# Feed-forward network: all gate and up slabs first, then the down projection by output chunk

## The chip, the core and the metric

The kernel runs on one core of one Trainium2 chip, in one launch. The metric is the device time of that launch in microseconds. The engines are TensorE (PE, matrix products into PSUM), VectorE (DVE), ScalarE (ACT), GpSimd (POOL) and SyncE (SP), which here only issues transfers. TensorE's weight loads have a row of their own in the profile (PEld).

## What is computed

Three transformer layers on one sequence of 256 tokens, width 1024, all in float32. The first has a stick-breaking and a differential attention side by side, the second a forgetting attention, the third a low-rank attention; each ends with the same feed-forward network, and the third is followed by a last normalization. The change touches only the three feed-forward networks:

```python
D_MODEL, SEQ = 1024, 256
D_FF = ((8 * D_MODEL // 3 + 255) // 256) * 256        # 2816 = 22 chunks of 128
def swiglu(xn, w_gate, w_up, w_down):
    return (jax.nn.silu(xn @ w_gate) * (xn @ w_up)) @ w_down
h = h + swiglu(rmsnorm(h, ffn_norm[l]), w_gate[l], w_up[l], w_down[l])
...
return rmsnorm(h, final_norm)
```

## The kernel before

**Slabs.** All weights lie in HBM as a row of slabs of 128 partitions x 1024 float32 (512 KB), numbered in the order of their use. Each slab goes through four steps: SyncE loads it into one of six slots of `stage`; ScalarE rounds it to a high part `w_hi` (`split_hi`, L1016, or `next_hi`, L1032); VectorE subtracts to get the low part `w_lo` (`split_lo`, `next_lo`, L1485); TensorE multiplies (L426). Activations are kept transposed, features on partitions and 256 tokens along the row, and are split in the same way, high and low. One block of 128x128 weights needs three products of 256 columns: high by high, high by low, low by high. Where the two parts of the activations stand side by side (`a_pair`), the first two are one product of 512 columns; its two halves come out in the two halves of a PSUM bank and are added later (`wide_slab`). The other form (`by_weights`) adds all three into the same 256 columns.

**Order of the work.** The order on each engine is written out by hand; engines wait for each other by counting semaphores: `loaded` (a transfer has landed), `hi_made`, `lo_made`, `slab_done` (TensorE is done with a slab). The load of slab n waits for `lo_made` of slab n-6, since they share a slot of `stage`. ScalarE's split of slab n+6 waits for `slab_done` of slab n, VectorE's low split that is written beside slab n is that of slab n+4.

**The feed-forward network.** 66 slabs in 11 rounds of six: gate, up, gate, up, down, down. A gate slab holds the weights of one of 22 chunks of 128 hidden features, for all 1024 inputs; an up slab the same. After them ScalarE copies out the low half of the bank (`low_out`, L1219), VectorE adds the halves (L1688) and multiplies by the row factor `rB` of the normalization (L1478), ScalarE does the silu (L1210), VectorE multiplies by the up part, and the result is split again (`ff_high`, L1214, `ff_low`, L1485). A down slab holds the 128 rows of one chunk, for all 1024 outputs: it adds into all eight output chunks, which stay in four PSUM banks (`acc`, banks 0 to 3) for the whole network (`row_slab`). Only two gated chunks exist at a time. The rounds 1 to 9 are loops on the engines (`Fori`), the first and the last are written out. At the end VectorE adds the eight sums to `xT` (L1515) and makes the low parts of the next stage's input, ScalarE its high parts (`norm_start`); TensorE begins the next stage's first two slabs block by block as these come in (`first_column_slabs`).

Of the kernel before, what the change touches and what calls it, by code (L numbers as in the profile page):

```python
# [18 lines left out]
P = 128  # L19
TOK = 256  # L20
D = 1024
NC = D // P
DFF = ((8 * D // 3 + 255) // 256) * 256
NG = DFF // 256
# [62 lines left out]
MLA_LAST = 14  # L87


def trunk(nc, xT_d, slab_d, vec_d, con_d, pos_d, out_d):  # L90
    f32, f32r, i32 = mybir.dt.float32, mybir.dt.float32r, mybir.dt.int32
    ALU, ACT = mybir.AluOpType, mybir.ActivationFunctionType
    with ExitStack() as ctx:
# [5 lines left out]

        stage = sb("stage", [P, SLOTS, SLAB])  # L100
# [5 lines left out]
        arena = sb("arena", [P, 10240])  # L106
# [24 lines left out]
        def chunks(t, a, n):  # L131
# [18 lines left out]
        ff_hi, ff_lo = chunks(arena_r, 0, 2), chunks(arena_r, 512, 2)  # L150
# [48 lines left out]
                                 "do_taken", "dms_done", "dr_ready", "dn_ready", "do_hi", "do_lo"))  # L199
        mix_ready, mhi_ready, mlo_ready = sem("mix_ready"), sem("mhi_ready"), sem("mlo_ready")  # L200
# [16 lines left out]
        fin_made, pool_added = sem("fin_made"), sem("pool_added")  # L217
# [106 lines left out]
        outT, gained, squared = chunks(arena, 0, 8), chunks(arena, 2048, 8), chunks(arena, 4096, 8)  # L324
# [6 lines left out]
        def _(sp):  # L331
# [33 lines left out]
            def ffn_loads(base, first=0):  # L365

                for n in range(base, base + 5):
                    load(n, n - first)
                with sp.Fori(0, NG - 1) as i:
                    for c, shift in enumerate((1, 1, -2, 0, 0, 0)):  # L370
                        n = base + 5 + c
                        sp.wait_ge(lo_made, i * SLOTS + (n + 1 - SLOTS))
                        sp.dma_start(stage[:, n % SLOTS, :],
                                     slab_d[bass.ds(i * SLOTS + (n + shift - first), 1)].rearrange("a p n -> p (a n)")
                                     ).then_inc(loaded[n % SLOTS], 16)
                load(base + 6 * NG - 1, base + 6 * NG - 1 - first)
# [40 lines left out]
            for i, (c, count) in enumerate(OUT_PARTS[:-1]):  # L417
                sp.wait_ge(out_ready, i + 1)
                sp.dma_start(out_d[:, c:c + count, :], outT[:, c:c + count, :]).then_inc(out_done, 16)
# [4 lines left out]
        def _(pe):  # L424
# [337 lines left out]
            def ff(p):  # L762
                return ff_hi[:, p, :], ff_lo[:, p, :]

            def ffn_round(f, base, i, last=False):

                n, q = base - 1 + 6 * i, 22 * f + 2 * i
                slot = [(base - 1 + c) % SLOTS for c in range(6)]
                for p in range(2):
                    pe.wait_ge(gu_taken, q + p - 1)  # L770
                    wide_slab(n + 3 * p, slot[3 * p], bank[4 + 2 * p])
                    pe.wait_ge(ff_made, q + p - 1)
                    if last and p:
                        column_slab(n + 4, slot[4], half(7, 0))
                    else:
                        wide_slab(n + 3 * p + 1, slot[3 * p + 1], bank[5 + 2 * p])
                    if p == 0:
                        pe.wait_ge(fflo_ready, q)
                        row_slab(n + 2, slot[2], *ff(1), False)
                if last:  # L780
                    last_rows(n + 5, [ff(0), ff(1)],
                              *([(done, q + 1), (done, q + 2)] for done in (ffhi_ready, fflo_ready)))
                    return
                pe.wait_ge(fflo_ready, q + 1)
                row_slab(n + 5, slot[5], *ff(0), False)

            def ffn(f, base):
                q = 22 * f
                if f:
                    pe.wait_ge(ff_made, q)  # L790
                first_column_slabs(base, [half(4, 0), half(5, 0)], 2 * f + 1)
                norm_sum(2 * f + 1)
                wide_slab(base + 2, (base + 2) % SLOTS, bank[6])
                pe.wait_ge(r_ready, 2 * f + 2)
                wide_slab(base + 3, (base + 3) % SLOTS, bank[7])
                pe.wait_ge(fflo_ready, q + 1)
# [194 lines left out]
            pe.wait_ge(ff_made, 22 * 3)  # L991
            for i, pair in enumerate((sumsq[:, :], sq[:, 0:TOK])):
                pe.wait_ge(fin_added, i + 1)
                mm(half(7, 0), ones, pair, i == 0)
            pe.wait_ge(pool_added, 1)
            mm(half(7, 0), ones, sq[:, TOK:2 * TOK], False)
            for c in (6, 7):
                pe.wait_ge(fin_squared, c + 1)
                last = mm(half(7, 0), ones, squared[:, c, :], False)
            last.then_inc(sum_done, 1)  # L1000
# [3 lines left out]
        def _(act):  # L1004
# [13 lines left out]
            def next_hi(n):  # L1018
                m = n + SLOTS
                if m < NSLAB:  # L1020
                    act.wait_ge(slab_done, n + 1)
                    act.wait_ge(loaded[m % SLOTS], 16 * (m // SLOTS + 1))
                    if m in UQ_STEP:
                        step = UQ_STEP[m]
                        if step[0] == "R":
                            for i in (m + 1, m + 2):
                                act.wait_ge(loaded[i % SLOTS], 16 * (i // SLOTS + 1))
# [34 lines left out]

            def norm_start(m):

                for c in range(NC):
                    act.wait_ge(x_ready, 8 * (m - 1) + c + 1)
# [1182 lines left out]
```

## Time and profile before

| | us |
|---|---|
| median of 3 runs | 1009.96 (1009.61 to 1009.97) |
| profiled execution, span | 1007.6 |
| TensorE busy | 993.9 (99%) |
| TensorE weight loads | 923.4 (92%) |
| VectorE busy | 714.1 (71%) |
| ScalarE busy | 607.8 (60%) |
| queue of SyncE's transfers | 52.9% of 16 engines |

The median of the runs lies 2.4 us above the span of the profiled execution. Busy time counts instructions in flight; TensorE's products overlap, so its own progress is read from the start times in its timeline. "Share" of a DMA queue is the time that its packets took, over the time of all 16 DMA engines. TensorE's granted clock is full (1.0) over the whole run but for the last microseconds.

### The profile page before, as it was taken

Reading aid. Unit: us, or ns where it says so; the run is one execution under the profiler, and the core shown is the slowest. Engines: PE = TensorE matmul, PEld = TensorE weight load, DVE = VectorE, ACT = ScalarE, POOL = GpSimd, SP = SyncE. Lnnn points to the kernel's source line nnn. Section 1 sums busy time; section 2 is a strip of 40 time slices with the busy share of each in tenths; the row PEclk is TensorE's granted clock in tenths of the full one; section 3 lists DMA queues with packets and bytes.
Section 4 is the critical chain, followed back from the end, with each engine's and each line's share of the span. In section 5 each row is a group of like instructions: output and inputs, shape, how many; then the busy total and the mean of one; then the engine's idle time right before and its main releaser. Section 6 shows DMA issues by size and latency. Waiting matters only on the chain.

```text
span 1007.6 us, 19765 instructions
## 1 busy us (share of the span) xinstructions
PE 993.9 (99%) x7214; PEld 923.4 (92%) x7214; DVE 714.1 (71%) x1360; ACT 607.8 (60%) x1094; POOL 59.6 (6%) x79
## 2 busy tenths in 40 slices
PE   8999999999999999999999999999999999999997
PEld 8999989999999999989999999999989999999996
DVE  4668987776666668666496666668977686666665
ACT  5677785575555556565475555557768675555553
POOL 3011110120000002000020000002200010000000
PEclk9999999999999999999999999999999999999999
DMA  7743445466555554433545556564665456565631
GB/s 292 273 149 110 153 145 187 148 206 190 176 181 186 183 189 159 157 127 127 167 146 188 187 187 187 187 187 127 203 194 191 146 167 188 187 187 187 187 125 43
DMA packets 50904, 174.05 MB, mean 173 GB/s; under 512 B 6304, under 2 KB 8864, under 8 KB 50720
## 3 DMA queue, kind: packets, MB, share of 16 engines
q1 hardware_dynamic: 49664, 172.12, 52.9%
q10 hardware_dynamic: 1184, 1.18, 0.6%
q8 instruction: 36, 0.59, 0.2%
q14 instruction: 20, 0.16, 0.0%
HBM read 169.86 MB, written 1.05 MB: 170 GB/s over the span
## 4 chain that ended last, share of the span: by engine, by line
PE 90%; DVE 5%; ACT 2%; DMA 1%; issue 1%; SPq 0%; DVEq 0%; ACTq 0%
PE bank L426 89%; DVE w_lo L1485 2%; PE bank L647 1%; DVE a_pair L1504 1%; DMA stage<-slab_dram 1%; DVE xT L1515 1%; DVE arena L1478 0%; ACT w_hi L1032 0%; ACT a_pair L1067 0%; DVE soft_s L1566 0%; ACT soft_p L1124 0%; ACT w_hi L1016 0%; DVE tmp L1478 0%; DVE tmp L1712 0%; DVE arena_r L1485 0%
## 5 line engine op out<-in xcount | busy, mean ns | idle before, releaser
L426 PE MATMUL bank<-a_pair,w_hi 128*128 128x256 f32 (+1 forms) x1992 | 537.8, 342 | 2.8 <-DVE w_lo L1485 2.7
L426 PE MATMUL bank<-a_pair,w_lo 128*128 128x256 f32 x1488 | 417.6, 282 | 0.0
L1485 DVE TENSOR_TENSOR w_lo<-stage,w_hi 128x1024 fp32r<-128x1024 f32 (+2 forms) x322 | 387.4, 1211 | 8.4 <-ACT w_hi L1016 3.5
L426 PEld LDWEIGHTS bank<-a_pair,w_hi 128*128 128x128 f32 x1992 | 343.4, 190 | 48.6 <-DVE w_lo L1485 4.0
L426 PE MATMUL bank<-arena_r,w_hi 128*128 128x256 f32 x1792 | 328.8, 284 | 0.4 <-DVE arena_r L1485 0.2
L426 PEld LDWEIGHTS bank<-arena_r,w_hi 128*128 128x128 f32 x1792 | 278.4, 191 | 5.6 <-DVE arena_r L1485 1.4
L426 PEld LDWEIGHTS bank<-a_pair,w_lo 128*128 128x128 f32 x1488 | 283.1, 190 | 0.0
L426 PE MATMUL bank<-arena_r,w_lo 128*128 128x256 f32 x896 | 252.7, 283 | 0.0
L1016 ACT ACTIVATE w_hi<-stage 128x1024 fp32r<-128x1024 f32 x192 | 202.4, 1055 | 33.4 <-PE bank L426 33.4
L1032 ACT ACTIVATE w_hi<-stage 128x1024 fp32r<-128x1024 f32 (+2 forms) x126 | 128.0, 1026 | 79.5 <-PE bank L426 69.7
L426 PEld LDWEIGHTS bank<-arena_r,w_lo 128*128 128x128 f32 x896 | 171.0, 191 | 0.0
L1688 DVE TENSOR_TENSOR tmp<-bank,arena 128x256 f32<-128x256 f32 x123 | 51.9, 422 | 160.3 <-ACT arena L1219 160.3
L1219 ACT ACTIVATE arena<-bank 128x256 f32<-128x256 f32 x123 | 47.1, 383 | 163.2 <-PE bank L426 163.2
L2088 POOL TENSOR_TENSOR sumsq<-sumsq,sq 128x256 f32<-128x256 f32 x47 | 38.5, 820 | 644.3 <-ACT sq L1053 591.8
L1478 DVE TENSOR_TENSOR tmp<-tmp,rB 128x256 f32<-128x256 f32 x129 | 54.4, 422 | 4.8 <-ACT tmp L1210 2.7
L1214 ACT ACTIVATE arena_r<-tmp 128x256 fp32r<-128x256 f32 x66 | 27.6, 418 | 43.5 <-DVE tmp L1478 35.7
L426 PE MATMUL bank<-w_hi,a_pair 128*128 128x256 f32 x256 | 47.7, 287 | 0.0
L426 PEld LDWEIGHTS bank<-w_hi,a_pair 128*128 128x128 f32 x256 | 39.8, 191 | 0.9 <-issue 0.6
L426 PE MATMUL bank<-w_lo,a_pair 128*128 128x256 f32 x128 | 36.2, 282 | 0.0
L1566 DVE CUSTOM_DVE_ANT_0 soft_s<-bank,con 128x128 f32<-128x128 f32 x80 | 25.1, 355 | 15.5 <-PE bank L426 15.4
L1154 ACT ACTIVATE soft_p<-soft_s,small 128x128 f32<-128x128 f32 x64 | 31.2, 491 | 4.0 <-DVE small L1619 3.2
L1504 DVE SCALAR_TENSOR_TENSOR a_pair<-xT,vec,a_pair 128x256 fp32r<-128x256 f32 x48 | 28.7, 604 | 6.5 <-ACT a_pair L1282 5.1
(185 smaller groups left out, 674.8 us busy)
## 6 DMA issues: line engine op xcount, KB each, us to landing
stage<-slab_dram SPq DMA_DIRECT2D x319, 512.0 KB, 4.2
con<-con_dram SPq DMA_DIRECT2D x1, 1153.5 KB, 10.6
xT<-xT_dram SPq DMA_DIRECT2D x4, 256.0 KB, 5.5
arena<-arena ACTq DMA_DIRECT2D x1, 1024.0 KB, 8.9
arena<-tmp SPq DMA_DIRECT2D x32, 32.0 KB, 3.2
out_dram<-arena SPq DMA_DIRECT2D x3, 256.0 KB, 2.4
tmp<-arena SPq DMA_DIRECT2D x16, 16.0 KB
vec<-vec_dram SPq DMA_DIRECT2D x1, 213.5 KB, 11.5
```

Source lines behind the costliest of these rows:

```text
L426: return nc.tensor.matmul(out, lhsT, rhs, start=start, stop=True, skip_group_check=True)
L1016: nc.scalar.activation(w_hi[:, slot, :], stage[:, slot, :], ACT.Copy).then_inc(hi_made, 1)
L1032: nc.scalar.activation(hi, raw, ACT.Copy).then_inc(hi_made, 1)
L1154: last = nc.scalar.activation(soft_p[:, g % 2, cols], soft_s[:, g % 2, cols], ACT.Exp, scale=0.125 if g < HEADS else rq_col[:, t:t + 1], b ...
L1214: nc.scalar.activation(ff_hi[:, p, :], tmp[:, 4 + p, :], ACT.Copy).then_inc(ffhi_ready, 1)
L1219: nc.scalar.activation(low[:, i, :], half(4 + (0, 2, 1, 3)[i], 1), ACT.Copy).then_inc(low_taken, 1)
L1478: return nc.vector.tensor_tensor(out, a, b, ALU.mult)
L1485: return nc.vector.tensor_tensor(out, a, hi.bitcast(f32), ALU.subtract)
L1504: return nc.vector.scalar_tensor_tensor(out, x, g, hi.bitcast(f32), ALU.mult, ALU.subtract)
L1566: return nc.vector.tensor_tensor_reduce(out=s[:, cols], in0=b[:, cols], in1=con[:, mask + cols.start:mask + cols.stop], scale=1.0, scalar= ...
L1688: return nc.vector.tensor_tensor(out, half(b, 0), low[:, i, :], ALU.add)
L2088: nc.gpsimd.tensor_tensor(sumsq[:, :], sumsq[:, :], sq[:, (i % 2) * TOK:(i % 2 + 1) * TOK], ALU.add).then_inc(sq_added, 1)
```

## The change

Each feed-forward network now runs its 44 gate and up slabs one after another, in eight PSUM banks in turn (`GU_BANK`), and keeps all 22 gated chunks, high and low part side by side (`ff_pair`): 12 in `arena_r`, 10 in `ff_more`, which lies over `arena`. The down projection then runs output chunk by output chunk: 8 columns of 22 blocks, each block one product of 512 columns and one of 256. The very last column of the third network keeps the three products of 256. The weights in HBM are laid out as before. A slab of eight down blocks is put together by the transfers: each block is 128 rows of 128 numbers (512 B) out of a different row slab, and 22 such slabs take 38 transfers. After each column VectorE adds the two halves of its bank to `xT`, and ScalarE and VectorE make the next stage's input for that chunk while the next column runs. The loops on the engines are gone.

```diff
+NF = 2 * NG
+GU_BANK = (4, 5, 6, 0, 1, 2, 3, 7)
+DOWN_BANK = (4, 0, 1, 2, 3, 7, 5, 6)
+DOWN = 2 * NF
+DOWN_END = {(NF * c + NF - 1) // NC: c for c in range(NC)}
+KEPT = 12
...
+        def down_order(c):
+            if c:
+                return [*range(0, NF, 2), *range(1, NF, 2)]
+            return [*range(0, NF - 2, 2), *range(1, NF - 2, 2), NF - 2, NF - 1]
...
             def ffn_loads(base, first=0):
-                for n in range(base, base + 5):
-                    load(n, n - first)
-                with sp.Fori(0, NG - 1) as i:
-                    for c, shift in enumerate((1, 1, -2, 0, 0, 0)):
...
+                for t in range(DOWN):
+                    load(base + t, base - first + 6 * (t // 4) + t % 4)
+                rows = slab_d[base - first:base - first + 6 * NG].rearrange("(i s) p n -> p i s n", s=6)
+                for s in range(NF):
+                    n = base + DOWN + s
+                    sp.wait_ge(lo_made, n - SLOTS + 1)
+                    for c, j, k, count in down_runs(s):
+                        sp.dma_start(
+                            span(stage[:, n % SLOTS, :], k * P, count * P).rearrange("p (i n) -> p i n", n=P),
+                            rows[:, j // 2:j // 2 + count, 4 + j % 2, c * P:c * P + P]).then_inc(loaded[n % SLOTS], 16)
...
+            def down_columns(f, base):
+                for c in range(NC):
+                    b = bank[DOWN_BANK[c]]
+                    plain = f == 2 and c == NC - 1
...
+                    for i, j in enumerate(down_order(c)):
+                        s, k = divmod(NF * c + i, NC)
+                        n, w = base + DOWN + s, slice(k * P, k * P + P)
+                        if k == 0:
+                            pe.wait_ge(lo_made, n + 1)
...
+                        if plain:
+                            last = by_weights(n % SLOTS, k * P, b[:, 0:TOK], ff_hi(j), ff_lo(j), i == 0)
+                        else:
+                            mm(b[:, :], w_hi[:, n % SLOTS, w], ff_pair(j), i == 0)
+                            last = mm(b[:, 0:TOK], w_lo[:, n % SLOTS, w], ff_hi(j), False)
...
             def ffn(f, base):
-                q = 22 * f
+                q = NF * f
                 if f:
                     pe.wait_ge(ff_made, q)
                 first_column_slabs(base, [half(4, 0), half(5, 0)], 2 * f + 1)
                 norm_sum(2 * f + 1)
-                wide_slab(base + 2, (base + 2) % SLOTS, bank[6])
-                pe.wait_ge(r_ready, 2 * f + 2)
-                wide_slab(base + 3, (base + 3) % SLOTS, bank[7])
-                pe.wait_ge(fflo_ready, q + 1)
-                row_slab(base + 4, (base + 4) % SLOTS, *ff(0), True)
-                with pe.Fori(1, NG - 1) as i:
-                    ffn_round(f, base, i)
-                ffn_round(f, base, NG - 1, last=True)
+                for t in range(2, DOWN):
+                    if t == 7:
+                        pe.wait_ge(r_ready, 2 * f + 2)
+                    if t >= 8:
+                        pe.wait_ge(ff_made if t % 2 else gu_taken, q + t // 2 - 3)
+                    wide_slab(base + t, (base + t) % SLOTS, bank[GU_BANK[t % 8]])
+                down_columns(f, base)
...
+                for j in range(1, NF):
+                    gate(f, j)
+                    ff_low(f, j - 1)
+                    next_lo(base + 2 * j)
+                    silu_out(f, j)
+                    up(f, j)
+                    next_lo(base + 2 * j + 1)
+                ff_low(f, NF - 1)
+                for s in range(NF):
+                    c = DOWN_END.get(s)
+                    if c is not None:
+                        down_residual(f, base, c)
+                    next_lo(base + DOWN + s)
+                    if c is not None and f < 2:
+                        norm_low(2 * f + 2, c)
```

TensorE, before, in the loop of the first network: the last block of an up slab and the start of the down slab behind it.

```order
1135 L426 MATMUL bank<-a_pair,w_hi 128x512
1136 L426 MATMUL bank<-a_pair,w_lo 128x256
1137 L784 REGISTER_ALU
1138 L487 REGISTER_ALU
1139 L426 MATMUL bank<-arena_r,w_hi 128x256 x2
1140 L426 MATMUL bank<-arena_r,w_lo 128x256
1141 L426 MATMUL bank<-arena_r,w_hi 128x256 x2
1142 L426 MATMUL bank<-arena_r,w_lo 128x256
```

TensorE, now, at the end of the 44th gate/up slab of the first network and the start of the first down column (`arena_r` holds the first twelve gated chunks, `ff_more` the others).

```order
1672 L479 MATMUL bank<-a_pair,w_hi 128x512
1673 L479 MATMUL bank<-a_pair,w_lo 128x256
1674 L479 MATMUL bank<-arena_r,w_hi 128x512
1675 L479 MATMUL bank<-arena_r,w_lo 128x256
...
1684 L479 MATMUL bank<-arena_r,w_hi 128x512
1685 L479 MATMUL bank<-arena_r,w_lo 128x256
1686 L479 MATMUL bank<-ff_more,w_hi 128x512
1687 L479 MATMUL bank<-ff_more,w_lo 128x256
```

A block of down weights was three products of 256 columns and is one of 512 and one of 256.

SyncE's queue, before, in the loop of the first network: one load per slab.

```order
35 L373 ISA
36 L373 DMA stage<-slab_dram 128x1024
37 L373 ISA
38 L373 DMA stage<-slab_dram 128x1024
39 L369 REGISTER_ALU
40 L369 COMPARE_AND_BRANCH
41 L353 DMA stage<-slab_dram 128x1024 x38
```

SyncE's queue, now, where the down slabs of the first network begin (partitions x blocks x numbers).

```order
20 L406 DMA stage<-slab_dram 128x1024 x64
21 L427 DMA stage<-slab_dram 128x8x128
22 L427 DMA stage<-slab_dram 128x2x128
23 L427 DMA stage<-slab_dram 128x6x128
24 L427 DMA stage<-slab_dram 128x4x128
25 L427 DMA stage<-slab_dram 128x128 x2
26 L427 DMA stage<-slab_dram 128x2x128
27 L427 DMA stage<-slab_dram 128x8x128
```

A down slab is no longer 128 rows of 4 KB but eight blocks of 128 rows of 512 B, in one to four transfers.

## Rows read from the trace of the kernel before

**Rows 1.** Page: engines (busy us, share, instructions); chain by engine and line.
```profile
PE 993.9 (99%) x7214; PEld 923.4 (92%) x7214; DVE 714.1 (71%) x1360; ACT 607.8 (60%) x1094; POOL 59.6 (6%) x79
...
PE bank L426 89%; DVE w_lo L1485 2%; PE bank L647 1%; DVE a_pair L1504 1%; DMA stage<-slab_dram 1%; DVE xT L1515 1%; DVE arena L1478 0%; ACT w_hi L1032 0%; ACT a_pair L1067 0%; DVE soft_s L1566 0%; ACT soft_p L1124 0%; ACT w_hi L1016 0%; DVE tmp L1478 0%; DVE tmp L1712 0%; DVE arena_r L1485 0%
```
**Rows 2.** TensorE's timeline: start, us, engine line op, tiles, shapes, count.
```profile
604.81 0.40 PE L426 MATMUL bank<-arena_r,w_hi 128*128 128x256 f32 x2
...
607.68 0.40 PE L426 MATMUL bank<-a_pair,w_hi 128*128 128x512 f32 x1
...
613.34 0.40 PE L426 MATMUL bank<-arena_r,w_hi 128*128 128x256 f32 x2
```
**Rows 3.** TensorE's timeline, start and end of FFN 1, start of FFN 2.
```profile
199.33 0.28 PE L426 MATMUL bank<-a_pair,w_hi 128*128 128x256 f32 x1
...
205.34 0.58 PE L426 MATMUL bank<-a_pair,w_hi 128*128 128x512 f32 x1
...
211.35 0.51 PE L426 MATMUL bank<-arena_r,w_hi 128*128 128x256 f32 x2
...
214.33 0.40 PE L426 MATMUL bank<-a_pair,w_hi 128*128 128x512 f32 x1
...
387.79 0.28 PE L426 MATMUL bank<-a_pair,w_hi 128*128 128x256 f32 x1
...
513.35 0.50 PE L426 MATMUL bank<-a_pair,w_hi 128*128 128x512 f32 x1
...
519.44 0.50 PE L426 MATMUL bank<-arena_r,w_hi 128*128 128x256 f32 x2 [0.18 <-DVE arena_r L1485]
```
**Rows 4.** Stretch 390 to 395: each engine's busy us (instructions), clock, DMA share, GB/s.
```profile
390.00:395.00 5.00, 5.00 (x44) 4.92 (x44) 4.97 (x7) 4.87 (x9) 2.74 (x4) 1.00 0.00 0
```
**Rows 5.** Timeline of all engines, the tail; in brackets the idle time before.
```profile
998.78 0.75 DVE L1515 TENSOR_TENSOR xT<-xT,bank 128x256 f32<-128x256 f32 x2 [0.35 <-PE bank L426]
...
999.95 1.03 PE L426 MATMUL bank<-arena,con 128*128 128x256 f32 x4
1001.01 0.47 ACT L1036 ACTIVATE rB<-bank,con 128x256 f32<-128x256 f32 x1 [0.23 <-PE bank L426]
```
**Rows 6.** Groups by line and shape: busy us, mean ns of one, idle before.
```profile
L1485 DVE TENSOR_TENSOR w_lo<-stage,w_hi 128x1024 fp32r<-128x1024 f32 x305 | 373.2, 1231 | 6.4 <-ACT w_hi L1016 3.5 <-ACT w_hi L1032 2.6
...
L1016 ACT ACTIVATE w_hi<-stage 128x1024 fp32r<-128x1024 f32 x192 | 202.4, 1055 | 33.4 <-PE bank L426 33.4
...
L1688 DVE TENSOR_TENSOR tmp<-bank,arena 128x256 f32<-128x256 f32 x123 | 51.9, 422 | 160.3 <-ACT arena L1219 160.3
...
L1219 ACT ACTIVATE arena<-bank 128x256 f32<-128x256 f32 x123 | 47.1, 383 | 163.2 <-PE bank L426 163.2
...
L1515 DVE TENSOR_TENSOR xT<-xT,bank 128x256 f32<-128x256 f32 x48 | 19.0, 413 | 14.3 <-PE bank L426 14.3
```
**Rows 7.** Page, DMA issues: KB of one, median us from issue to landing.
```profile
stage<-slab_dram SPq DMA_DIRECT2D x319, 512.0 KB, 4.2
```
**Rows 8.** DMA by stretch (packets, MB, share of engines); 0:3, 17:19, 19:21, 211:399, 727:739.
```profile
GB/s 0 0 0 0 0 0 0 0 0 0 0 0 0 0 0 0 0 0 0 0 0 0 0 0 51 68 85 82 28 72 79 55 218 273 218 273 273 300 300 191
...
DMA packets 373, 0.78 MB, mean 388 GB/s; under 512 B 43, under 2 KB 250, under 8 KB 373
q1 hardware_dynamic: 373, 0.78, 105.1%
...
DMA packets 223, 0.82 MB, mean 410 GB/s; under 512 B 26, under 2 KB 26, under 8 KB 222
q1 hardware_dynamic: 222, 0.80, 100.1%
...
DMA packets 9371, 34.16 MB, mean 182 GB/s; under 512 B 1042, under 2 KB 1042, under 8 KB 9368
q1 hardware_dynamic: 9368, 34.11, 57.8%
...
q10 hardware_dynamic: 1040, 1.05, 49.9%
```

More of the change, by code:

```diff
@@ L149, in trunk @@
         ob_hi, ob_lo = chunks(arena_r, 2048, 4), chunks(arena_r, 3072, 4)
[L150 removed]
+        ff_first = span(arena_r, 0, KEPT * 2 * TOK).rearrange("p (c n) -> p c n", n=2 * TOK)
         fo_hi, fo_lo = chunks(arena_r, 0, 8), chunks(arena_r, 2048, 8)
@@ L322, in add_index, with ff_pair, ff_hi, ff_lo @@
             return 7 * m + (6 if m > 4 else 0)
-        outT, gained, squared = chunks(arena, 0, 8), chunks(arena, 2048, 8), chunks(arena, 4096, 8)
+        gained, squared = chunks(arena, 5120, 8), chunks(arena, 7168, 8)
+        def ff_pair(j):
+            return ff_first[:, j, :] if j < KEPT else ff_more[:, j - KEPT, :]
+        def ff_hi(j):
+            return ff_pair(j)[:, 0:TOK]
+        def ff_lo(j):
+            return ff_pair(j)[:, TOK:2 * TOK]
+        def down_order(c):
+            if c:
+                return [*range(0, NF, 2), *range(1, NF, 2)]
+            return [*range(0, NF - 2, 2), *range(1, NF - 2, 2), NF - 2, NF - 1]
+        def down_runs(s):
+            runs = []
+            for k in range(NC):
+                c, i = divmod(NC * s + k, NF)
+                j = down_order(c)[i]
+                if runs and runs[-1][0] == c and runs[-1][1] + 2 * runs[-1][3] == j:
+                    runs[-1][3] += 1
+                else:
+                    runs.append([c, j, k, 1])
+            return runs
+        def loads_of(n):
+            s = [n - base - DOWN for base in (FFN1, FFN2, FFN3) if base + DOWN <= n < base + 6 * NG]
+            return len(down_runs(s[0])) if s else 1
+        def all_loads(n):
+            return 16 * sum(loads_of(m) for m in range(n % SLOTS, n + 1, SLOTS))
+        def column_ended(engine, f, base, c):
+            if c in (3, 7):
+                engine.wait_ge(slab_done, base + DOWN + (NF * (c + 1)) // NC)
+            else:
+                engine.wait_ge(down_done, 6 * f + c + 1 - c // 4)
         OUT_PARTS = ((0, 1), (1, 2), (3, 2), (5, 2), (7, 1))
@@ L990, in _ @@
             ffn(2, FFN3)
[L991 to L1000, printed above, removed]
+            pe.wait_ge(fin_added, NC - 2)
+            mm(half(7, 0), ones, sumsq[:, :], True)
+            pe.wait_ge(fin_squared, NC)
+            mm(half(7, 0), ones, squared[:, NC - 1, :], False).then_inc(sum_done, 1)
         @block.scalar
@@ L1455, in _ @@
             ffn(2, FFN3)
-            for c in range(NC):
-                act.wait_ge(x_ready, 8 * 5 + c + 1)
-                nc.scalar.activation(squared[:, c, :], xT[:, c, :], ACT.Square).then_inc(fin_squared, 1)
-                for i in {5: (0,), 7: (6, 7)}.get(c, ()):
-                    nc.scalar.activation(gained[:, i, :], xT[:, i, :], ACT.Copy, scale=gain(6, i)).then_inc(fin_made, 1)
             norm_end(6)
@@ new lines, in ff_low, with ffn @@
+            def ff_low(f, j):
+                dve.wait_ge(ffhi_ready, NF * f + j + 1)
+                minus_hi(ff_lo(j), tmp[:, 4 + j % 2, :], ff_hi(j)).then_inc(fflo_ready, 1)
+            def ffn(f, base):
+                next_lo(base)
+                next_lo(base + 1)
+                dve.wait_ge(r_ready, 2 * f + 2)
+                plain_gate(base, NF * f)
+                silu_out(f, 0)
+                plain_up(base + 1, NF * f)
+                for j in range(1, NF):
[6 more added lines that the diff above has]
+                ff_low(f, NF - 1)
+                for s in range(NF):
+                    c = DOWN_END.get(s)
+                    if c is not None:
+                        down_residual(f, base, c)
+                    next_lo(base + DOWN + s)
+                    if c is not None and f < 2:
+                        norm_low(2 * f + 2, c)
+                    if c is not None and f == 2 and c < NC - 1:
+                        dve.wait_ge(x_ready, 8 * 5 + c + 1)
+                        nc.vector.tensor_scalar(gained[:, c, :], xT[:, c, :], gain(6, c), None, ALU.mult
+                                                ).then_inc(fin_gained, 1)
+                        add_square(c)
```

267 lines of the change are left out of this document (93 added, 174 removed).

## The prediction

> **What bounds the kernel now.** I read the page first, then TensorE's timeline, then the DMA view in stretches, then the engines' groups by shape. The page shows one bound: TensorE is busy for 99% of the span, and the chain of waits runs over its product line for 89% of it [rows 1]. In TensorE's timeline the FFN is a strict beat. A gate or up slab (eight 512-column products and eight of 256) starts at 607.68, two of them last until 613.34: 5.66 us, 2.83 each. A down slab (24 products of 256 columns) starts at 604.81 and lasts until 607.68: 2.87 us, and over the whole loop a round of two gate/up slabs and one down slab is 8.53 us, so 2.88 fits better than 2.87 [rows 2]. So both forms stream the same 768 columns for each weight block, and the wide form costs 0.05 us less per slab. The first FFN takes 199.33 to 387.79, 188.46 us [rows 3].
>
> Nothing else is on the path there. At the hand-over from the first FFN to the next stage (390 to 395) TensorE is busy for all 5.00 us although VectorE and ScalarE are full and no load moves [rows 4]. So the end-of-FFN residuals are already hidden, and taking them out of that place gives no time.
>
> **The change part by part.**
>
> 1. Down slabs in the wide form. 66 slabs (22 in each of three FFNs), 0.05 us each: 3.3 us. The very last column keeps the old form, 22 blocks x 0.36 instead of 0.353: 0.15 us back. Three up slabs that were plain (24 products) become wide: 0.15 us. Sum 3.3 us gained.
>
> 2. The first down slab no longer stands behind the first gated chunk. In before, slabs 3 and 4 take 205.34 to 211.35, 6.01 us where two wide slabs take 5.66; the next slab takes 2.98 where 2.88 is usual [rows 3]. So 0.35 + 0.1 us is a wait for the first chunk's low part. In after the fifth slab is a gate slab that wants only its weights. The second FFN shows 513.35 to 519.44, 6.09 us, in the same place [rows 3], and the third the same. Gain 3 x 0.45 to 0.55: 1.4 us.
>
> 3. The tail. In before the two last residual adds stand in a row from 998.78, then the square and the closing product at 999.95, and ScalarE starts on the norm at 1001.01 [rows 5]. In after only one output chunk waits for the last slab: one add of about 0.4 us less. Gain 0.4 us.
>
> 4. VectorE. For each pair of gate/up slabs it makes two low splits (2 x 1.23 us), five products or sums of 256 columns and one low part of the chunk, 0.42 us each: 2.46 + 2.52 = 4.98 us [rows 6], beside 5.66 us of TensorE. Before, a down slab came in between and gave it 8.53 us for 6.2. It is 88% full now, so it keeps up, with 0.68 us for its waits. I take zero. The low split it has to deliver is for the slab four further on, over 8 us away, so a single late step is absorbed; only a mean over 5.66 would cost. ScalarE has 2 x 1.06 + 2 x 0.38 [rows 6] and two more of about 0.42: 3.7 us, loose. In the down phase VectorE gets 16 adds of 0.41 us [rows 6] and 8 low parts per FFN, while its 22 splits take 27 of the 62 us: hidden. PSUM: a bank is used again after eight slabs, and what frees it is asked for three chunks back; no wait. The residuals that go away from the hand-over were hidden (above): zero.
>
> 5. The transfers. This is where the change can lose. A gate/up slab still moves in 128 pieces of 4 KB. A down slab is now 1024 pieces of 512 B, in 38 transfers for 22 slabs. The issue costs nothing: fewer than two a slab, and one transfer of 1024 pieces of 1 KB (arena to arena) is already there. What one slab may take is TensorE's 2.83 us, since the loads go one behind another. A load is issued when the slab six earlier has been split and is wanted about 8 us later in the gate/up phase; with 4.2 us from issue to landing [rows 7] about 4 us are spare, once per FFN. So the loss per FFN is 22 x (L - 2.83) - 4 us, L being one slab's transfer, and nothing when that is negative.
>
> L is not in the trace. Its nearest rows: from 19 to 21 the queue is full with 4 KB pieces and moves 410 GB/s; from 17 to 19 it is as full, with 330 data pieces (373 less 43 small) of 2.36 KB on average, most of them 1 to 1.7 KB, and moves 388 GB/s [rows 8]. On 16 engines that is 160 ns for 4096 B and 97 ns for 2364 B: 0.036 ns per byte and 12 ns for each piece. A piece of 512 B comes to 31 ns, 64 per engine to 2.0 us. In the FFN itself the queue is occupied 57.8% for 182 GB/s, that is 315 GB/s when occupied and not 410 [rows 8], so the same stretch by 1.3: 2.6 us. I take L = 2.6 us: under 2.83, hidden, with 8% of room. The low end, bytes alone, is 512 KB at 410 GB/s: 1.3 us. The high end is the arena-to-arena transfer: 1040 pieces of 1 KB occupy 49.9% of 16 engines for 12 us, 92 ns each [rows 8]. If that price went with the piece and not with the byte, 64 of them are 5.9 us.
>
> The Trainium skill (DMA: Bandwidth & Descriptors, Why small descriptors are slow) gives a fixed cost of about 3 cycles per packet beside one per 32 bytes: 19 cycles for 512 B, against 131 for 4 KB, so 16% more for a slab. By that rule, scaled from the 1.3 us of the rows, L would be 1.5 us; the two windows make it 2.0, so the trace finds more cost than the rule.
>
> Sum: 3.3 + 1.4 + 0.4 = 5.1 us. The profiled span is 1007.6; the median of the runs is 1009.96, 2.4 us above it, and I keep that distance. Span 1002.5, time 1004.9 us.
>
> **Rivals.**
>
> A. Pieces are supplied no faster than one per 3 to 4 ns, whatever their size. For: the very first transfer (128 pieces of 256 B) runs at 51 to 85 GB/s with the engines far from full [rows 8], 3.0 ns a piece at best and about 3.9 in the mean (32 KB in 0.5 us). Against: it is the first one, cold, and 1 KB pieces ran back to back. Then L is 3.1 to 4.0; with 3.5 the loss is 3 x (22 x 0.67 - 4) = 32 us: 1037 us. It decides from L = 3.1, where the loss (2 us per FFN) eats the gain. TensorE would idle in the down phase, waiting for VectorE's low split, which waits for ScalarE's split, which waits for the load. The same holds if scattered reads of one 512 B column out of 4 KB rows lower the memory's rate by a third or more.
> [...]
>
> B. The arena price, L = 5.9: 3 x (22 x 3.07 - 4) = 191 us: 1196 us. Against: that transfer reads and writes on-chip memory at the same time, the new ones only write it.
>
> C. VectorE becomes the bound in the gate/up phase: its order (gate, low part, split, rescale, up, split) waits for ScalarE twice per pair. If each pair takes one ScalarE split more (1.06 us), a pair is 6.0 and not 5.66: 21 x 3 x 0.35 = 22 us: 1027 us. Against: ScalarE is busy 3.7 of 5.66.
>
> D. No change: small stalls of the first down slabs give the 5 us back: 1009 to 1011 us.
>
> **How the numbers follow.** Forecast (1003 to 1008) 0.58; A 0.26, of which a third lies above 1040; B 0.03; C 0.05; D 0.08. What a measurement of this kernel can tell from no change is about 0.2%, 2 us. Faster 0.60 (the forecast and the smallest part of A), same 0.09, slower 0.31. The forecast's own range is 1003 to 1008; the range that holds 8 in 10 goes up into A: 1002.5 to 1040.
>
> **What would show it.** Right: in the down phase TensorE's 512- and 256-column products alternate without a gap, 2.83 us per slab; the DMA share there rises from 0.58 towards 0.9; issue to landing of the 512 B slabs under 8 us; each FFN about 186.8 us. Wrong by A: VectorE's low split as TensorE's releaser and, behind it, ScalarE waiting on the slab load, a DMA share near 1 (or a rate near 3 ns per piece with a lower share). Wrong by C: low splits late in the gate/up phase, where the loads are old ones.

## The result, and the profile after

The changed kernel takes 1001.17 us (median of 4 runs, 1000.99 to 1002.94) against 1009.97 us (1009.61 to 1010.71): a ratio of 0.9917, 95% interval 0.9903 to 0.9931. Forecast were 1004.9 us, range 1002.5 to 1040: the sign was right, the gain was 8.8 us and not 5.1, and the time lies 1.3 us below the range. The profiled execution has a span of 999.5 us at a time of 1001.25.

The page of the changed kernel, engines and chain, which answers to [rows 1]:

```profile
PE 985.7 (99%) x6678; PEld 893.9 (89%) x6678; DVE 736.7 (74%) x1392; ACT 594.7 (59%) x1095; POOL 58.1 (6%) x78
...
PE 95%; DVE 2%; ACT 1%; DMA 1%; issue 0%; SPq 0%; DVEq 0%; ACTq 0%
```

TensorE is still the bound, with fewer products. TensorE's timeline of the changed kernel where stages begin (start, us, then the instruction; answers to [rows 3]): `a_pair` at 128x256 opens an FFN (feed-forward network) or the stage behind it, `arena_r` at 128x512 the down columns, `sumsq` the tail.

```profile
199.27 0.28 PE L479 MATMUL bank<-a_pair,w_hi 128*128 128x256 f32 x1
...
321.94 0.39 PE L479 MATMUL bank<-arena_r,w_hi 128*128 128x512 f32 x1
...
382.95 0.28 PE L479 MATMUL bank<-a_pair,w_hi 128*128 128x256 f32 x1
...
502.11 0.28 PE L479 MATMUL bank<-a_pair,w_hi 128*128 128x256 f32 x1
...
627.32 0.40 PE L479 MATMUL bank<-arena_r,w_hi 128*128 128x512 f32 x1
...
689.50 0.28 PE L479 MATMUL bank<-a_pair,w_hi 128*128 128x256 f32 x1
...
802.83 0.28 PE L479 MATMUL bank<-a_pair,w_hi 128*128 128x256 f32 x1
...
990.80 0.59 PE L479 MATMUL bank<-sumsq,con 128*128 128x256 f32 x2
```

The same starts in the kernel before, as far as [rows 3] doesn't have them:

```profile
506.95 0.28 PE L426 MATMUL bank<-a_pair,w_hi 128*128 128x256 f32 x1
...
695.88 0.28 PE L426 MATMUL bank<-a_pair,w_hi 128*128 128x256 f32 x1
...
809.26 0.28 PE L426 MATMUL bank<-a_pair,w_hi 128*128 128x256 f32 x1
...
998.59 0.38 PE L426 MATMUL bank<-sumsq,con 128*128 128x256 f32 x1
```

Differences of such starts, in both traces:

| stage | before, us | after, us | saved |
|---|---|---|---|
| FFN 1 | 188.46 | 183.68 | 4.78 |
| second layer's attention | 119.16 | 119.16 | 0 |
| FFN 2 | 188.93 | 187.39 | 1.54 |
| third layer's attention | 113.38 | 113.33 | 0.05 |
| FFN 3 | 189.33 | 187.97 | 1.36 |
| tail | 9.0 | 8.7 | 0.25 |

The sum is 8.0 of the 8.1 us by which the spans differ. The second and third FFN save about what was forecast (some 1.6 each). The first saves 3.3 us more. Its down phase takes 61.01 us (321.94 to 382.95) where the second's takes 62.18 (627.32 to 689.50), with the same instructions. The reason is in the smallest rows. First the changed kernel in FFN 1 and in FFN 2, TensorE's timeline:

```profile
259.54 0.39 PE L479 MATMUL bank<-a_pair,w_hi 128*128 128x512 f32 x1
259.77 0.28 PE L479 MATMUL bank<-a_pair,w_lo 128*128 128x256 f32 x1
259.89 0.39 PE L479 MATMUL bank<-a_pair,w_hi 128*128 128x512 f32 x1
...
520.26 0.40 PE L479 MATMUL bank<-a_pair,w_hi 128*128 128x512 f32 x1
520.50 0.28 PE L479 MATMUL bank<-a_pair,w_lo 128*128 128x256 f32 x1
520.61 0.40 PE L479 MATMUL bank<-a_pair,w_hi 128*128 128x512 f32 x1
520.84 0.28 PE L479 MATMUL bank<-a_pair,w_lo 128*128 128x256 f32 x1
520.96 0.40 PE L479 MATMUL bank<-a_pair,w_hi 128*128 128x512 f32 x1
```

Then the kernel before, the same view, in the first two wide slabs of FFN 1 and in a loop round of FFN 2:

```profile
206.91 0.39 PE L426 MATMUL bank<-a_pair,w_hi 128*128 128x512 f32 x1
207.14 0.28 PE L426 MATMUL bank<-a_pair,w_lo 128*128 128x256 f32 x1
207.26 0.39 PE L426 MATMUL bank<-a_pair,w_hi 128*128 128x512 f32 x1
...
608.04 0.40 PE L426 MATMUL bank<-a_pair,w_hi 128*128 128x512 f32 x1
608.28 0.28 PE L426 MATMUL bank<-a_pair,w_lo 128*128 128x256 f32 x1
608.40 0.40 PE L426 MATMUL bank<-a_pair,w_hi 128*128 128x512 f32 x1
```

A wide block (512 and 256 columns) has two beats, a beat being the distance from the start of one block to the start of the next. In the fast one it is 346.7 ns throughout (mean of 510 blocks of FFN 1; 230 ns from the start of the wide product to that of the narrow one, then 117). In the slow one the mean is 353.3 ns (998 blocks of FFN 2 and 3), in a cycle of three blocks, about 350, 361 and 349. The record of the 512-column product shows it at a glance: 0.39 us in the fast beat, 0.40 in the slow one. In the kernel before all loop rounds have the slow beat, which is the 2.83 us per slab that I read from [rows 2]; only the first two wide slabs of FFN 1 have the fast one. The granted clock is the same, as the stretches of the changed kernel show (from:to, length, busy us and instructions of PE, PEld, DVE, ACT, POOL, then clock, DMA share, GB/s): two of gate/up slabs in FFN 1 and 2, one of down columns.

```profile
213.00:321.00 108.00, 108.00 (x625) 95.25 (x624) 91.34 (x160) 64.31 (x119) 0.00 (x0) 1.00 0.63 191
329.00:382.00 53.00, 53.00 (x308) 46.73 (x307) 33.25 (x40) 25.34 (x33) 4.77 (x6) 1.00 0.68 202
517.00:625.00 108.00, 108.00 (x613) 93.64 (x612) 89.54 (x154) 62.65 (x116) 0.00 (x0) 1.00 0.63 190
```

TensorE is "busy" for all 108 us in both stretches and does 625 products in one, 613 in the other: 2% that neither TensorE's busy share nor the clock shows. (The granted clock was 0.5 from 7.9 to 11.3 us and in the last microseconds, in both kernels and outside all three FFNs.)

The waits of FFN 1 in the changed kernel (210 to 382), the costliest three (us in total, times, longest):

```profile
POOL sumsq L2099 <- ACT sq L1102: 165.5, 6, 131.5
ACT arena L1270 <- PE bank L479: 44.1, 40, 1.4
DVE xT L1560 <- PE bank L479: 18.9, 7, 3.6
```

None of that view's rows has TensorE as the one that waits; at the start of FFN 2 its weight load waits once for a low split, 0.4 us. VectorE is 85% busy in the gate/up phase (91.34 of 108) and late for nothing. The tail, all engines' timeline (answers to [rows 5]), now has one add:

```profile
991.00 0.42 DVE L1561 TENSOR_TENSOR xT<-xT,bank 128x256 f32<-128x256 f32 x1 [6.13 <-PE bank L479]
...
992.66 0.47 ACT L1085 ACTIVATE rB<-bank,con 128x256 f32<-128x256 f32 x1 [0.39 <-PE bank L479]
```

The transfers while only down slabs are loaded (325 to 360) and the page's row on a whole slab (answers to [rows 7]):

```profile
DMA packets 13554, 6.80 MB, mean 194 GB/s; under 512 B 336, under 2 KB 13552, under 8 KB 13552
...
q1 hardware_dynamic: 13552, 6.77, 69.6%
...
stage<-slab_dram SPq DMA_DIRECT2D x277, 512.0 KB, 4.0
```

The queue is occupied 0.696 x 35 us for 6.77 MB: 1.89 us for a slab of 0.524 MB. (The loads run ahead of TensorE: in a window up to 380 a third of the bytes would be the next stage's 4 KB pieces.)

### The profile page after: what moved, and what is told of

Read it like the earlier page. It is cut to its first block, busy times and chain, and to the rows that moved or that the text cites. A ratio compares the mean times of both kernels' runs of the same rounds, so it can differ in the third digit from the quotient of the medians.

```text
span 999.5 us, 17282 instructions
## 1 busy us (share of the span) xinstructions
PE 985.7 (99%) x6678; PEld 893.9 (89%) x6678; DVE 736.7 (74%) x1392; ACT 594.7 (59%) x1095; POOL 58.1 (6%) x78
## 4 chain that ended last, share of the span: by engine, by line
PE 95%; DVE 2%; ACT 1%; DMA 1%; issue 0%; SPq 0%; DVEq 0%; ACTq 0%
PE bank L479 94%; PE bank L700 1%; DMA stage<-slab_dram 1%; DVE w_lo L1512 1%; DVE arena L1505 0%; ACT w_hi L1081 0%; DVE soft_s L1601 0%; ACT soft_p L1175 0%; DVE soft_p L1629 0%; DVE arena L1872 0%; ACT arena L1096 0%; DVE arena L1905 0%; ACT arena L1095 0%; DVE soft_p L1625 0%; DVE arena L1870 0%
## 5 line engine op out<-in xcount | busy, mean ns | idle before, releaser
L479 PE MATMUL bank<-a_pair,w_hi 128*128 128x512 f32 (+1 forms) x1968 | 533.7, 343 | 2.2 <-DVE w_lo L1512 2.1
L1081 ACT ACTIVATE w_hi<-stage 128x1024 fp32r<-128x1024 f32 (+2 forms) x314 | 326.5, 1044 | 140.0 <-PE bank L479 128.0
L479 PE MATMUL bank<-arena_r,w_hi 128*128 128x256 f32 (+1 forms) x1036 | 239.1, 315 | 0.0
L479 PE MATMUL bank<-arena_r,w_lo 128*128 128x256 f32 x656 | 184.6, 282 | 0.0
L479 PEld LDWEIGHTS bank<-arena_r,w_hi 128*128 128x128 f32 x1036 | 170.1, 190 | 14.0 <-issue 1.4
L479 PEld LDWEIGHTS bank<-arena_r,w_lo 128*128 128x128 f32 x656 | 125.0, 191 | 0.0
L479 PE MATMUL bank<-ff_more,w_hi 128*128 128x512 f32 (+1 forms) x250 | 86.5, 387 | 0.0
L479 PE MATMUL bank<-ff_more,w_lo 128*128 128x256 f32 x240 | 67.4, 281 | 0.0
L479 PEld LDWEIGHTS bank<-ff_more,w_hi 128*128 128x128 f32 x250 | 46.3, 188 | 10.3
L479 PEld LDWEIGHTS bank<-ff_more,w_lo 128*128 128x128 f32 x240 | 45.4, 189 | 0.0
```

The source lines that it names most:

```text
L479: return nc.tensor.matmul(out, lhsT, rhs, start=start, stop=True, skip_group_check=True)
L1081: nc.scalar.activation(hi, raw, ACT.Copy).then_inc(hi_made, 1)
```

## The experiments

**The transfers alone.** `e1_rows4k` keeps everything but loads a down slab as 128 whole rows (the down weights are then the wrong ones, the amount of work is the same).

```diff
-                    for c, j, k, count in down_runs(s):
-                        sp.dma_start(
-                            span(stage[:, n % SLOTS, :], k * P, count * P).rearrange("p (i n) -> p i n", n=P),
-                            rows[:, j // 2:j // 2 + count, 4 + j % 2, c * P:c * P + P]).then_inc(loaded[n % SLOTS], 16)
+                    sp.dma_start(stage[:, n % SLOTS, :], rows[:, s // 2, 4 + s % 2, :]).then_inc(loaded[n % SLOTS], 16)
```

> The changed kernel, but each down slab is loaded as whole rows of 4 KB in one transfer (the down weights of a block are then wrong ones; the work on all engines is the same). If the gathered transfers are hidden, 1001.2 us as the changed kernel, within 1 us. If they cost something, or if the 8 us gained come partly from lighter memory traffic, it differs by more than 2 us; my prediction's rival A (pieces are supplied at 3 to 4 ns each) would make this one faster by several us.

Measured: 1001.3 us (997.28, 1001.49, 1001.41, 1001.18), the time of the changed kernel. The run of 997.28 is the profiled one, and in it FFN 2 has the fast beat too (625 products in 517 to 625). It lies some 4 us below the other three: one FFN is 510 blocks x 6.6 ns = 3.4 us, and most of the rest is in the third layer's attention, 112.65 us here and 113.33 in the changed kernel. Its transfers from 325 to 360:

```profile
q1 hardware_dynamic: 1899, 6.89, 62.3%
```

That is 1.66 us per slab. The pieces of 512 B cost 0.23 us of queue per slab and nothing in time.

**The product form alone.** `e2_down256` keeps the new order and transfers, and gives every down column the three products of 256.

```diff
-                    plain = f == 2 and c == NC - 1
+                    plain = True
...
-                if f < 2 or c < NC - 1:
-                    chain(nc.vector.tensor_tensor(xT[:, c, :], xT[:, c, :], half(DOWN_BANK[c], 1), ALU.add))
```

> The changed kernel, but every down column in three products of 256 columns (one add per column at its end). My theory of two beats (a wide block takes 346.7 ns in one state of TensorE, 353.3 in another, and the first FFN of the changed kernel was in the fast one): the first FFN loses 22 x 8 x 13.3 ns = 2.3 us, the others 154 and 176 blocks x 6.7 ns = 1.2 and 1.0 us: 1005.7 us. The prediction's single price of 0.05 us a slab: 1001.2 + 3.1 = 1004.3 us. Rival, the gain is in the gate and up slabs standing together and not in the form: no difference, 1001 us.

Measured: 1005.13 us (1003.13 to 1006.79), ratio 0.9959 (0.9945 to 0.9973), so the form is worth some 4 us of the 8.8. The two expectations with a gain from the form, 1004.3 and 1005.7 us, both lie within the spread of the runs; it only excludes that the form gains nothing. In the profile (1003.13) the down columns of FFN 2 run from 629.99 to 693.35: 176 blocks in 63.36 us, 360 ns each, without spread and with no fast or slow variant. Against them the changed kernel's wide columns take 62.18 (slow) or 61.01 (fast). The gate/up slabs of FFN 1 are fast here too: FFN 1 takes 186.02 us, 2.4 less than before with the down weights in the old form. So most of that FFN's surplus comes from the gate/up slabs standing together. In this profile those of FFN 3 are fast as well, worth 336 blocks x 6.6 ns = 2.2 us.

**The loops.** `e3_before_straight` is the kernel before with its loops written out on all engines (TensorE's edit; the others are alike).

```diff
-                with pe.Fori(1, NG - 1) as i:
+                for i in range(1, NG - 1):
                     ffn_round(f, base, i)
```

> The kernel before, its loops on the engines written out. Theory of two beats: the row form (256, 256, 256) ahead of each gate slab puts TensorE into the slow beat each time, loop or not, so 1010 us as before. Rival, the loops' branches and registers cost the 6.6 ns per wide block: 42 x 3 x 8 x 6.6 ns = 6 us less, about 1003 us.

Measured: 1009.94 us over 10 runs against 1009.41, ratio 1.0008 (0.9999 to 1.0018), and the slow beat in all the rounds behind the first (only the two wide slabs ahead of FFN 1's and FFN 2's first down slab are fast). Neither the loops nor their branches cost time, and they don't bring the slow beat.

**What flips the beat.** `e4_probe` puts, ahead of six gate slabs per FFN, one or two more products of various widths into the bank that the slab then starts anew.

```diff
...
+                for cols in extra:
+                    mm(out[:, 0:cols], w_hi[:, slot, 0:P], a_pair[:, 0, 0:cols], True)
```

> The changed kernel with extra products of 32 to 512 columns ahead of some gate slabs (every sixth slab of each FFN), into the bank that the slab is about to start, so without effect on the result. Each adds 0.05 to 0.5 us of its own. Two beats as a state that an interruption can change: the beat of the wide blocks (512 plus 256 columns) flips between 346.7 and 353.3 ns behind some of the sizes, in the first FFN from fast to slow and in the others from slow to fast. Rival, the beat belongs to the FFN (its addresses, its code, its traffic): no flip, 346.7 in the first and 353.3 ns in the others throughout.

Measured: 999.50 us, one run. In the trace, F for 346.7 and S for 353.3 ns from there to the next: FFN 1 begins F, then 256 F, 128 **S**, 64 F, 512 F, 192 F, 384 F. FFN 2 begins S, then 256 S, 128 S, 64 **F**, 512 **S**, 192 S, 384 **F**. FFN 3 begins F, then 256+256 F, 320 F, 32 F, 448 F, 128+128 **S**, 96 **F**. One extra product of 64 columns, TensorE's timeline of that kernel in FFN 2:

```profile
555.14 0.40 PE L479 MATMUL bank<-a_pair,w_hi 128*128 128x512 f32 x1
555.38 0.28 PE L479 MATMUL bank<-a_pair,w_lo 128*128 128x256 f32 x1
555.50 0.50 PE L479 MATMUL bank<-a_pair,w_hi 128*128 128x64 f32 x2
555.85 0.28 PE L479 MATMUL bank<-a_pair,w_lo 128*128 128x256 f32 x1
```

The rival is excluded. The beat is a state that in these traces changes only where something breaks the alternation, and not each time; it goes through from the gate/up slabs into the down columns. The extra costs 0.11 us: 555.50 to 555.85 is 0.35 where a 512-column product takes 0.24.

**One extra product per FFN.** `e5_settle` is the changed kernel with a 64-column product ahead of the fifth gate/up slab of each FFN.

```diff
+                if settle:
+                    mm(out[:, 0:64], w_hi[:, slot, 0:P], a_pair[:, 0, 0:64], True)
...
-                    wide_slab(base + t, (base + t) % SLOTS, bank[GU_BANK[t % 8]])
+                    wide_slab(base + t, (base + t) % SLOTS, bank[GU_BANK[t % 8]], t == 4)
```

> The changed kernel with one extra product of 64 columns ahead of the fifth slab of each FFN (0.11 us each, no effect on the result). The probe showed that behind an extra product of 64 (twice), 32, 96 or 384 columns the beat was fast, whatever it was before. Theory of two beats: all three FFNs run at 346.7 ns per block to their end; two FFNs more in the fast beat give 2 x 500 x 6.6 ns = 6.6 us less than a run with one of them fast: 994.8 us, and the runs agree more closely. Rival, the beat of FFN 2 and 3 is drawn anew by something that comes later than this: 1001 us on the mean, runs between 994 and 1004.

Measured: 995.38 us (995.12, 998.96, 994.99, 997.71, 995.38), ratio 0.987 (0.9851 to 0.9888): 5.8 us below the changed kernel by the medians, and the fastest of all here. The stretches of all three FFNs (gate/up) have the fast beat's count:

```profile
213.00:321.00 108.00, 108.00 (x625) 1.00 0.64 191
517.00:625.00 108.00, 108.00 (x625) 1.00 0.65 192
815.00:922.00 107.00, 107.00 (x620) 1.00 0.65 192
```

FFN 2 enters slow and is fast from the extra on (514.9), FFN 3 from 812.8. The FFNs take 183.80, 184.20 and 184.91 us, so the second and third are 3.2 and 3.1 us shorter than in the changed kernel, as 494 and 472 blocks x 6.67 ns, less 0.11 for the extra, demand (3.2 and 3.0). Bringing the fast beat to the other two FFNs gains in each what FFN 1 had beyond them: this shows the beat as the cause of the surplus. Two of the five runs lie 2.6 and 3.8 us above the lowest group, so the runs don't agree more closely, as the expectation had it.

**The same extra in the kernel before.** `e6_before_settle` has it at each gate slab behind a down slab, 20 per FFN, with the loops written out.

```diff
...
-                    wide_slab(n + 3 * p, slot[3 * p], bank[4 + 2 * p])
+                    wide_slab(n + 3 * p, slot[3 * p], bank[4 + 2 * p], True)
```

> The kernel before with its loops written out and one extra product of 64 columns ahead of each gate slab that follows a down slab (20 per FFN). Theory: the two wide slabs behind it run at 346.7 ns and not 353.3, 16 x 6.6 = 0.11 us less, for 0.11 us that the extra product costs: the time stays at 1009 to 1011 us and only the beat changes. Rival, the slow beat of the kernel before belongs to its banks or to VectorE's and ScalarE's reads: the beat stays 353.3 ns and the time rises by 6.6 us.

Measured: 1012.68 us, one run. In the trace the pairs of gate/up slabs are fast and slow in turn (fast from 223.2, 240.4, 257.5, slow between), which neither the theory nor its rival had. 60 extras x 0.11 us cost 6.6, some 30 pairs x 16 blocks x 6.6 ns give back 3.2: 3.4 us more than before, and 3 were measured. So the old order can run fast too, but there each down slab breaks the alternation and a single extra holds for 16 blocks only.

**Smaller pieces.** `e7_pieces256` halves each piece of the changed kernel's down slabs, 2048 of 256 B per slab.

```diff
...
-                            rows[:, j // 2:j // 2 + count, 4 + j % 2, c * P:c * P + P]).then_inc(loaded[n % SLOTS], 16)
+                        for h in (0, 64):
...
+                                rows[:, j // 2:j // 2 + count, 4 + j % 2, c * P + h:c * P + h + 64]
```

> The changed kernel with each 512 B piece of a down slab split into two of 256 B, 2048 pieces a slab. It asks how near the transfers are to the bound. By the per-piece price of 12 ns and 0.036 ns per byte, 128 x 21 = 2.7 us per slab, by the 1.3 for interruptions 3.5 us: 3 x (22 x 0.7 - 4) = 34 us slower, 1035 us. By what the changed kernel's trace shows for a 512 B slab (68% of 2.77 us occupied, 1.9 us), less 0.036 x 512 x 64 = 1.2 us for the bytes, 0.7 us is for 1024 pieces, so 2.6 us here: hidden, 1001 us. By a supply of one piece per 3 ns (rival A): 6 us a slab, 3 x (22 x 3.4 - 4) = 212 us slower.

Measured: 1001.48 us (1001.37, 998.12, 1001.59, 1001.75), no loss. Its transfers from 325 to 360:

```profile
DMA packets 27802, 6.98 MB, mean 200 GB/s; under 512 B 27799, under 2 KB 27799, under 8 KB 27799
...
q1 hardware_dynamic: 27799, 6.94, 102.5%
```

That is 2.71 us per slab, just under the 2.77 that TensorE takes (over 100% of share means that the times of packets overlap): the queue is full almost all the time, and these transfers are hidden with nothing to spare. So 4 KB, 512 B and 256 B pieces occupy the queue for 1.66, 1.89 and 2.71 us. The Trainium skill (DMA: Bandwidth & Descriptors, Why small descriptors are slow) counts 3 cycles per packet beside one per 32 bytes, 131, 19 and 11 cycles for these sizes: 16% and 34% more for a slab than with 4 KB. The runs find 14% and 63%: the rule fits at 512 B and is far too low at 256 B, where the queue is full.

**Another order of the same products.** `e8_pairs` gives two blocks of a gate/up slab as 512, 512, 256, 256 columns; the down columns keep the alternation.

```diff
+                for k in range(0, NC, 2):
+                    two = [(i, slice(i * P, i * P + P)) for i in (k, k + 1)]
+                    for i, w in two:
+                        mm(out[:, :], w_hi[:, slot, w], a_pair[:, i, :], i == 0)
+                    for i, w in two:
+                        last = mm(out[:, 0:TOK], w_lo[:, slot, w], a_hi[:, i, :], False)
```

> The changed kernel, its gate and up slabs in another order: 512, 512, 256, 256 columns for two blocks and not 512, 256, 512, 256. If the slow beat comes from a product of 512 columns that alternates with one of 256, this order has its own beat; at the floor of 13.3 ns beyond the columns of each product it is 693.3 ns for two blocks, 346.7 each, in every FFN: 994 to 996 us. If nothing depends on the order, the beats are as in the changed kernel, 346.7 in the first FFN and mostly 353.3 in the others, 1001 us.

Measured: 999.3 us, one run, above the 994 to 996 forecast. The gate/up blocks take 348.3 ns in all three FFNs (two blocks, first start to first start, halved), the down blocks 353.3 in all three. These two together are the miss: 1008 blocks x 1.6 ns and 506 x 6.6 ns are 5.0 us over an all-fast kernel.

**More extras.** `e9_settle4` has the 64-column product at four places, to catch a beat that goes slow again (the edit is against `e5_settle`).

```diff
-                    wide_slab(base + t, (base + t) % SLOTS, bank[GU_BANK[t % 8]], t == 4)
+                    wide_slab(base + t, (base + t) % SLOTS, bank[GU_BANK[t % 8]], t in (4, 17, 30, 43))
```

> As the kernel with one extra product of 64 columns per FFN, but with four of them (ahead of gate/up slabs 5, 18, 31 and 44), 9 x 0.11 = 1.0 us more of its own. Two of the five timed runs of that kernel were 2.5 to 3.5 us over the others. If in those an FFN fell out of the fast beat half way, four chances to come back make the runs agree: 995.5 to 997 us, none over 998. If the beat was not the reason, the spread stays (one or two of five runs 2 to 4 us over the rest) at a median of 996.4 us.

Measured: 1001.32 us (1000.47 to 1001.89), ratio 0.9918 (0.9904 to 0.9932): no better than with none, and the idea behind it fell. Its stretches in FFN 1's down columns, after the fourth extra, and in FFN 2 after the first, second and third:

```profile
330.00:382.00 52.00, 52.00 (x303) 1.00 0.68 199
517.00:551.00 34.00, 34.00 (x198) 1.00 0.65 200
554.00:588.00 34.00, 34.00 (x195) 1.00 0.59 187
591.00:625.00 34.00, 34.00 (x194) 1.00 0.63 184
```

The blocks are fast after the first, slow after the second and third, fast after the fourth, and alike in all three FFNs. So the extra doesn't bring the fast beat. With 64 columns all four cases occur: from slow to fast and fast to fast (`e5_settle`), from fast to slow and slow to slow (here). So the beat before doesn't decide alone which one follows. That the extra shifts a phase of the alternation fits this, but no run shows it. Three times 200 slow blocks x 6.6 ns are 4.0 us and the nine further extras 1.0: 995.1 + 5.0 = 1000.1, and the profiled run took 1000.48.

**The order in pairs everywhere.** `e10_pairs_all` has 512, 512, 256, 256 in the down columns as well.

```diff
...
                             mm(b[:, :], w_hi[:, n % SLOTS, w], ff_pair(j), i == 0)
-                            last = mm(b[:, 0:TOK], w_lo[:, n % SLOTS, w], ff_hi(j), False)
+                            if i % 2 == 0:
+                                first_of_two = w, j
+                                continue
+                            for v, q in (first_of_two, (w, j)):
+                                last = mm(b[:, 0:TOK], w_lo[:, n % SLOTS, v], ff_hi(q), False)
```

> The changed kernel with its products in the order 512, 512, 256, 256 (two blocks) in the gate/up slabs and in the down columns. With this order in the gate and up slabs alone those ran at 347.8 ns per block in all three FFNs, without a settling product, and the down columns at 353.3. If the order removes the slow beat, the down columns run at 347.8 ns too: 1514 blocks at 347.8 against 1514 at 351.4 in the changed kernel, 5.4 us less than 1001.2: 995.8 us, whatever the state at the start of an FFN. If the down columns have a slow beat of their own, 998 to 999 us.

Measured: 998.3 us (997.19, 997.75, 999.42, 998.85), ratio 0.9892 (0.9876 to 0.9908). In its profile all stretches of the FFNs, the down columns too, have 348.3 ns per block; two of gate/up slabs, FFN 1 and 2:

```profile
213.00:321.00 108.00, 108.00 (x622) 1.00 0.62 190
517.00:625.00 108.00, 108.00 (x622) 1.00 0.63 192
```

The 995.8 us of the expectation took 347.8 ns against 351.4. With 348.3 against the changed kernel's mean of 351.1 it is 4.2 us less, 997.0, and the profiled run took 997.19; no trace covers the slower ones. The order gives most of the fast beat in every FFN, 2.9 us below the changed kernel by the medians; `e5_settle` is 2.9 us faster still.

## Why the prediction was right in sign and short in size

**The step that failed is the first term's price.** It took "2.83 each" from [rows 2] as the one price of a wide slab and gave the gain as 66 slabs x 0.05 us. The wide block has two prices, and the new order of FFN 1 puts all its wide blocks (42 gate/up slabs, and 22 slabs' worth in the down columns) into the cheaper beat: 64 x 8 blocks less the 16 that were fast before, x 6.6 ns, are 3.3 us, the whole of what FFN 1 saved beyond the others. The rows I showed held a sign of it: [rows 3] has two wide slabs and a wait in 6.01 us, and I put all above 5.66 down to the wait. In the trace it is 0.53 us for the first block (205.34 to 205.87), 5.20 for fifteen at 346.7 ns and 0.28 of wait. That price got no range: the low end of 1002.5 left 2.4 us for all further gain, and the beat alone brought 3.3. The sign and the forecast's 5 us came from the right mechanism, but the time of 1001.2 also holds luck: FFN 2 entered slow here and fast in the profiled run of `e1_rows4k`, which took 997.28.

**Term 1, the form itself,** was right at the slow beat: `e2_down256` has 360 ns per block of three products against 353.3, so 506 down blocks x 6.7 ns = 3.4 us, forecast 3.3.

**Term 2, the wait for the first chunk,** was somewhat large. What is left of each FFN's saving is 4.78 - 3.3 - 1.17 = 0.3, 1.54 - 1.17 = 0.4 and 1.36 - 1.03 = 0.3 us, 1.0 in all against 1.4. In FFN 1 a part of what [rows 3] counted as wait was the long first block, which stays (205.27 to 205.81).

**Term 3, the tail:** 0.25 us against 0.4.

**The hand-over:** taking the residuals out of it gave nothing (0 and 0.05 us), as forecast.

**Term 4, VectorE:** right. It is 85% busy in FFN 1 where 88% was worked out, and TensorE's products wait for no low split in the FFNs.

**Term 5, the transfers:** hidden, as forecast, but L is 1.89 us, not 2.6, and the queue's share in the down phase 0.70, not near 0.9. The scaling by 1.3 was right for the bytes: for whole rows it makes 1.3 x 1.3 = 1.7 us, and they take 1.66. The price of 12 ns per piece, from the start-up stretch with its mixed sizes, was too high: the 56 further pieces per engine cost 0.23 us, 4 ns each.

**The rivals.** A (pieces supplied no faster than 3 to 4 ns) and B (the arena's price) are excluded: 2048 pieces moved in 2.71 us of queue, 1.3 ns each, and cost no time, and that is twice the pieces of the change. One piece of 512 B occupied its engine for 29 ns where B had 92. The scattered reads lowered the rate while the queue is occupied from 316 (whole rows) to 278 GB/s, by an eighth and not by a third. C is excluded by the waits, D by the interval of the ratio. With 0.31 on "slower", most of my doubt went to the transfers, and none to the side on which the result fell.

**The sum again:** 3.4 + 1.0 + 0.25 + 0.05, and 3.3 for the beat, is 8.0 of the span's 8.1. The other 0.6 to 0.7 us: the profiled time lies 1.75 us above its span, where I kept 2.4.

**What stays open.** What physically sets the two beats isn't shown. In the seven profiles with the new order and the alternation FFN 1 was fast at once in all, FFN 2 in two (`e1_rows4k`, `e9_settle4`) and FFN 3 in two (`e2_down256`, `e4_probe`). TensorE's weight load waits 0.4 us for a low split ahead of FFN 2 in the fast cases as in the slow ones, so that wait doesn't decide it. Which event does was not tried. Nor do the traces cover the slower runs of `e5_settle` (997.71 and 998.96): they lie where one FFN in the slow beat would put them, which is argued, not shown.

## What to carry to other kernels

Price a repeated group of products at every place where it occurs, by the mean distance of starts over many repeats, before one number is used for all: two prices for the same instructions mean that a reordering can move work from one to the other. A stretch in which an engine is 100% busy at full clock is not proof of full pace; count instructions in equal stretches. And where a transfer is hidden, its price decides nothing until it comes near the beat of the engine that covers it, so the doubt in a forecast belongs to the unit price of the bounding engine first.

## What the runs showed of the hardware

- A block of one 512- and one 256-column product has two stable beats at granted clock 1.00: 346.7 and 353.3 ns. 768 columns at 2.4 GHz are 320 ns; the fast beat is that and 2 x 13.3 ns, three products of 256 take 360, that and 3 x 13.3. So the fast beat fits the price per product that the three-product form shows, and the slow one adds 6.7 ns. The Trainium skill (TensorE: Matmul & The Clock Gate, Back-to-back issue gap) gives 2.5 ns beyond the columns for an isolated product. By that figure a block would take 325 ns, an estimate which no stretch reaches.
- An extra product of 64 columns (0.11 us) can flip the beat either way (`e4_probe`, `e9_settle4`); the order 512, 512, 256, 256 runs at 348.3 ns per block wherever it was used.
- A slab of 512 KB from HBM occupies the queue for 1.66 us in 4 KB pieces, 1.89 in 512 B and 2.71 in 256 B, at some 193 to 198 GB/s of demand; with 256 B the queue is full.
